# Sixteen feed-forward products ahead of the second group's norm, activations kept split for both column halves, last chunks staggered

## The reference, cut to what matters

```python
merged = sigmoid(ga) * (ya @ w_oa) + sigmoid(gb) * (yb @ w_ob)
x = x + merged @ w_out
h = rmsnorm(x, g_ffn)
a, u = split(h @ w_gu, 2, axis=-1)
x = x + (silu(a) * u) @ w_down
y = rmsnorm(x, g_final)
```

## Time and profile before

| | us |
|---|---|
| median of 3 runs (lowest, highest) | 1729.94 (1729.34, 1731.08) |
| the profiled execution | 1735.67 |
| its span, first to last instruction | 1733.9 |
| PE busy | 1653.6 (95%) |
| DVE busy | 953.3 (55%) |
| ACT busy | 662.3 (38%) |
| mean granted TensorE clock, share of full | 0.985 |

### The profile page before, as it was taken

The page is one execution under the profiler, slowest core; times in us unless marked ns, Lnnn a source line. Parts: engine busy times, 40 slices in busy tenths (PEclk is TensorE's granted clock), DMA queues, the critical chain, the costliest instruction groups (busy, mean ns, idle before and its releaser), DMA issues. The chain is left out here.

```text
span 1733.9 us, 27407 instructions
## 1 busy us (share of the span) xinstructions
PE 1653.6 (95%) x10688; PEld 1543.3 (89%) x10688; DVE 953.3 (55%) x2043; ACT 662.3 (38%) x1262; POOL 132.7 (8%) x235
## 2 busy tenths in 40 slices
PE   6999999999999999999998689999999999999997
PEld 6999999999999988888986689999999998787875
DVE  6546555654654634354564666666666664454444
ACT  5335444544544533342433422222222222334323
POOL 3001111000000001020010000000000002000000
PEclk9999999999999999999999889999999999999998
DMA  6142333455242345666461223222222228665643
GB/s 197 28 153 93 134 102 98 135 162 148 66 132 90 114 131 141 224 208 246 140 214 65 78 81 94 75 75 76 75 82 83 80 70 280 205 195 170 219 146 103
DMA packets 187824, 225.59 MB, mean 130 GB/s; under 512 B 13623, under 2 KB 135000, under 8 KB 187176
## 3 DMA queue, kind: packets, MB, share of 16 engines
q1 hardware_dynamic: 166608, 151.03, 29.2%
q0 software_dynamic: 21088, 72.81, 11.6%
HBM read 173.32 MB, written 50.54 MB: 129 GB/s over the span
## 5 line engine op out<-in xcount | busy, mean ns | idle before, releaser
L2021 PE MATMUL ps<-h_hi,w_hi 128*128 128x384 f32 (+1 forms) x816 | 275.0, 337 | 1.8 <-DVE w_lo L1366 1.1
L2023 PE MATMUL ps<-h_hi,w_lo 128*128 128x384 f32 (+1 forms) x816 | 267.9, 328 | 0.0
L2022 PE MATMUL ps<-h_lo,w_hi 128*128 128x384 f32 (+1 forms) x816 | 267.8, 328 | 0.0
L2021 PE MATMUL ps<-t_hi,e_hi 128*128 128x272 f32 x704 | 203.6, 289 | 10.6 <-DVE silu L1783 10.6
L2022 PE MATMUL ps<-t_lo,e_hi 128*128 128x272 f32 x704 | 203.6, 289 | 0.0
L2023 PE MATMUL ps<-t_hi,e_lo 128*128 128x272 f32 x704 | 202.8, 288 | 0.0
L2021 PE MATMUL ps<-b_hi,e_hi 128*128 128x272 f32 x528 | 155.0, 294 | 11.4 <-DVE e_lo L1768 11.4
L2021 PEld LDWEIGHTS ps<-h_hi,w_hi 128*128 128x128 f32 x816 | 155.1, 190 | 3.2 <-DVE w_lo L1366 1.4
L2022 PEld LDWEIGHTS ps<-h_lo,w_hi 128*128 128x128 f32 x816 | 155.0, 190 | 0.5 <-issue 0.5
L2023 PEld LDWEIGHTS ps<-h_hi,w_lo 128*128 128x128 f32 x816 | 154.6, 189 | 0.0
L2022 PE MATMUL ps<-b_lo,e_hi 128*128 128x272 f32 x528 | 154.3, 292 | 0.0
(11 more groups left out here) (320 smaller groups left out, 3554.4 us busy)
## 6 DMA issues: line engine op xcount, KB each, us to landing
w_raw<-in_w_gu_dram SPq DMA_DIRECT2D x96, 256.0 KB, 3.2
w_raw<-in_w_down_dram SPq DMA_DIRECT2D x88, 256.0 KB, 3.1
as_raw<-act_d SPq DMA_DIRECT2D x44, 512.0 KB, 4.7
w_raw<-in_w_in_dram SPq DMA_DIRECT2D x68, 256.0 KB, 3.3
zg_d<-stg POOLq DMA_DIRECT2D x28, 544.0 KB, 3.1
act_d<-act POOLq DMA_DIRECT2D x44, 272.0 KB, 2.7
w_raw<-in_w_out_dram SPq DMA_DIRECT2D x32, 256.0 KB, 3.7
gate<-zg_d POOLq DMA_DIRECT2D x8, 576.0 KB, 4.2
```

The costliest lines, as they stand in the source:

```text
L2021: nc.tensor.matmul(out, l_hi, r_hi, start=start, stop=False)
L2022: nc.tensor.matmul(out, l_hi, r_lo, start=False, stop=False)
L2023: return nc.tensor.matmul(out, l_lo, r_hi, start=False, stop=stop)
```

## The change

1. `FILL` goes from 4 to 8: sixteen products (P1 and P2 of f = 0 to 7) stand before P6 of f = 0. `p1` and `silu1` have eight buffers; to make room `sum2`, `sum3`, `col12`, `col22` have one each and `col21` goes (P4 adds straight into `act1`).
2. The sums of group 1's tiles are cut in pieces (`sums_first`, `sums_second`, `sums_hi(o, which)`, `sums_lo(o, which)`) and put between the sixteen products, one piece a product. The splits of products 2 and 3 stand ahead of the first tile's sums.
3. In `out_second` the turn of group 0's tile c stands in the middle of chunk c and its copies in iteration c; the left residual is added in two parts around the split of chunk 5.
4. Chunks 6 and 7 of w_out, and 42 and 43 of w_down, are staggered: chunk 6 of three tiles, chunk 7 of the same three, then both of the fourth and of the fifth.
5. `as_hi` and `as_lo` have eleven places and stay for the right half of the columns: 22 loads and splits of activations in place of 44.
6. `x1f`, `new_raw` and `gfin_row` are loaded behind given chunks of `ffn_out`, not in one burst; the split of `new_raw` moves from chunk 12 to 16.

```diff
-FILL = 4
-PRODUCTS = [("P1", 0), ("P1", 1), ("P2", 0), ("P2", 1), ("P1", 2), ("P1", 3), ("P2", 2), ("P2", 3)]
+FILL = 8
+PRODUCTS = [(_p, _f + _k) for _f in range(0, FILL, 2) for _p in ("P1", "P2") for _k in range(2)]
...
+def next_splits(q):
+    n = 2 * FILL
+    if n - RING <= q < n:
+        return {n - 3: (n,), n - 2: (n + 1, n + 2), n - 1: (n + 3,)}.get(q, ())
+    return (q + RING,) if q + RING < NQ else ()
...
 (POOL, ffn_out)
-            pool.wait_ge(sem("e_used"), NQ)
...
+            for t in range(4):
+                after_chunk(1 + 2 * t)
+                pool.dma_start(x1f[0][:, t, :], x1_d[t]).then_inc(sem("x1_landed0"), 16)
...
+                after_chunk(10 + k)
                 pool.dma_start(new_raw[:, :, 32 * k:32 * k + 32], act_d[:, :, HALF * k + 512:HALF * k + HALF].rearrange("b p t -> p b t")) \
...
+            for t in range(5):
+                after_chunk(12 + t)
...
 (ScalarE, end of out_second and ffn_in)
                 product_hi(0)
                 product_hi(1)
-                sums_hi(0)
-                std_d1(4)
+                sums_hi(0, range(4))
                 product_hi(2)
                 product_hi(3)
-                direct_hi(1)
-                product_read(0)
-                product_hi(4)
-                sums_hi(1)
...
+                std_d1(4)
...
+                beside = {0: lambda: direct_hi(1), 3: lambda: direct_hi(2), 7: lambda: direct_hi(3), 10: lambda: direct_hi(4)}
+                sums = {0: (1, (0, 1)), 1: (1, (2, 3)), 4: (2, (0, 1)), 5: (2, (2, 3)), 8: (3, (0, 1)), 9: (3, (2, 3)),
+                        11: (4, (0, 1)), 12: (4, (2, 3))}
+                for q in range(2 * FILL):
+                    if q in beside:
+                        beside[q]()
+                    if q in sums:
+                        sums_hi(*sums[q])
+                    for ahead in next_splits(q):
+                        product_hi(ahead)
+                    product_read(q)
...
 (VectorE, out_second)
                 for c in range(7):
-                    split_lo(b + c + 1, (c + 1) % 2)
-                    if 1 <= c < 5:
-                        operands_d0(c - 1)
-                    if 1 <= c < 3:
-                        scale_d0(c + 1)
                     if c == 4:
                         v.wait_ge(sem("x1_landed1"), 16 * 5)
-                        residual(1, 0, x1, D_BANKS[1], b + 4 - NB, "d1_x1")
+                        residual(1, 0, x1, D_BANKS[1], b + 4 - NB, "d1_x1", (0, 1))
+                    split_lo(b + c + 1, (c + 1) % 2)
+                    if c < 4:
+                        operands_d0(c)
+                    if c < 2:
+                        scale_d0(c + 2)
+                    if c == 4:
+                        residual(1, 0, x1, D_BANKS[1], b + 4 - NB, "d1_x1", (2, 3, 4))
...
 (VectorE, its end, and ffn_in)
                 product_lo(0)
                 product_lo(1)
-                sums_lo(0)
+                sums_lo(0, range(4))
                 scale_d1(2)
...
+                product_lo(2)
+                product_lo(3)
...
+                def beside(q):
+                    if q in (0, 4, 8, 11):
+                        sums_first((1, 2, 3, 4)[(0, 4, 8, 11).index(q)])
+                    elif q in (1, 5, 9, 12):
+                        o = (1, 2, 3, 4)[(1, 5, 9, 12).index(q)]
+                        sums_second(o)
+                        sums_lo(o, (0,))
+                    elif q in (2, 6, 10, 13):
+                        sums_lo((1, 2, 3, 4)[(2, 6, 10, 13).index(q)], (1, 2, 3))
+                    elif q in (3, 7):
+                        scale_d1(3 if q == 3 else 4)
...
+                for q in range(NQ):
+                    beside(q)
+                    if q and PRODUCTS[q - 1][0] == "P3":
+                        second_act(PRODUCTS[q - 1][1])
...
+                    product_read(q)
+                    for ahead in next_splits(q):
+                        if PRODUCTS[ahead][0] == "P6":
+                            weight_sums(PRODUCTS[ahead][1])
+                        product_lo(ahead)
...
 (ScalarE and VectorE, ffn_out)
-                        if m >= 1:
-                            act_hi(m + 1)
+                        if m and (m + 1) % 22 < 11:
+                            act_hi((m + 1) // 22, (m + 1) % 11)
...
 (TensorE)
-                pe.wait_ge(w_lo_done, CH_D[1] + 8)
-                for o, (t, R) in enumerate(last_tiles):
...
+                for o, c in ((0, 6), (1, 6), (2, 6), (0, 7), (1, 7), (2, 7), (3, 6), (3, 7), (4, 6), (4, 7)):
+                    pe.wait_ge(w_lo_done, CH_D[1] + c + 1)
...
-                turns_before = {0: 1, 2: 2, 5: 3, 7: 4}
+                turns_before = {0: 1, 2: 2, 5: 3, 9: 4}
...
+                for t, m in ((0, 42), (1, 42), (2, 42), (0, 43), (1, 43), (2, 43), (3, 42), (3, 43), (4, 42), (4, 43)):
+                    pe.wait_ge(w_lo_done, N_CHUNKS + m + 1)
```

More of the change, by code:

```diff
@@ L317, in build_program @@
         assert H0 - 16384 == H0 - 2 * 8192
[L318 to L334, removed]
@@ L335, in build_program, with temps @@
-        new_parts = place("new_parts", [P, NFF, P], F32R, at=H0 + 78336)
-        yf = place("yf", [P, 5, D], at=H0 + 89600)
-        gfin_row = place("gfin_row", [P, D], at=H0 + 110080)
+        def temps(name, places):
+            return [place(f"{name}_{k}", [P, 2, HALF // 2], at=H0 + at) for k, at in enumerate(places)]
+        p1 = temps("p1", (168192, 120832, 104448, 108800, 113152, 172544, 176896, 181248))
+        silu1 = temps("silu1", (170368, 123008, 106624, 110976, 115328, 174720, 179072, 117504))
@@ new lines, in build_program @@
+        sum2, sum3, col22, col12 = (temps(n, (142592 + 2176 * k,))[0] for k, n in enumerate(("sum2", "sum3", "col22", "col12")))
+        act1, act2 = (temps(n, (142592 + 2176 * (4 + 2 * k), 142592 + 2176 * (5 + 2 * k))) for k, n in enumerate(("act1", "act2")))
+        as_hi = place("as_hi", [P, 11, 2, 512], F32R, at=H0 + 8192)
+        as_lo = place("as_lo", [P, 11, 2, 512], F32R, at=H0 + 53248)
+        as_raw = place("as_raw", [P, 2, 2, 512], at=H0)
+        x1f = [place("x1f0", [P, 4, D], at=H0 + 98304), place("x1f1", [P, 5, D], at=H0 + 114688)]
@@ L339, in build_program @@
+        new_raw = place("new_raw", [P, NFF, DEC], at=H0 + 135168)
+        new_parts = place("new_parts", [P, NFF, P], F32R, at=H0 + 140800)
+        yf = place("yf", [P, 5, D], at=H0 + 152064)
+        gfin_row = place("gfin_row", [P, D], at=H0 + 180736)
         ps = ctx.enter_context(nc.psum_tensor("ps", [P, 8, 512], F32))
@@ L900, in _, with after_chunk @@
                         .then_inc(sem(f"act_saved{f % 2}"), 16)
-            pool.wait_ge(sem("e_used"), NQ)
[L902 to L906, removed]
+            def after_chunk(m):
+                pool.wait_ge(w_used, N_CHUNKS - NB - 2 + m + 1)
+            for t in range(4):
+                after_chunk(1 + 2 * t)
+                pool.dma_start(x1f[0][:, t, :], x1_d[t]).then_inc(sem("x1_landed0"), 16)
             for f in range(2):
@@ L1196, in direct_hi, with sums_hi @@
                     nc.scalar.copy(b22_hi[:, :, P * (o - 1):P * o], bank_view(bank + 1, P)).then_inc(sem("t_hi_done"), 1)
-            def sums_hi(o):
+            def sums_hi(o, which):
                 cols, w = (slice(512, HALF), 32) if o == 0 else (slice(P * (o - 1), P * o), P)
-                for k in range(4):
+                for k in which:
                     a.wait_ge(sem("t_sums"), T_SUMS[o] - 3 + k)
@@ L1247, in product_read @@
                     a.wait_ge(sem("e_read"), D_COUNT["P3", f])
-                    nc.scalar.activation(col12[f % 2][:, :, :], col12[f % 2][:, :, :], ACT.Silu).then_inc(sem("e_act_read"), 1)
+                    nc.scalar.activation(col12[:, :, :], col12[:, :, :], ACT.Silu).then_inc(sem("e_act_read"), 1)
             def out_first():
@@ L1868, in residual_tile, with residual @@
                 nc.vector.tensor_tensor(part, ps[0:R, bank, :], part, ALU.add).then_inc(sem(name), 1)
-            def residual(g, half, x1, banks, used, name):
+            def residual(g, half, x1, banks, used, name, tiles=None):
                 t0, nt = GROUPS[g][:2]
                 v.wait_ge(w_used, used)
-                for t in range(nt):
+                for t in tiles or range(nt):
                     residual_tile(x1, rows_of(t0 + t), t, half, banks[half][t], name)
@@ L2299, in tile_product, with token_chunk @@
                 return nc.tensor.matmul(ps[:, bank, :], l_hi, r_lo, start=False, stop=stop)
-            def token_chunk(banks, tiles, first, last_k, stationary, slot, wait=None):
+            def token_chunk(banks, tiles, first, last_k, stationary, slot, wait=None, between=None):
                 hi, lo = v2(w_hi, slot), v2(w_lo, slot)
                 for q in range(2):
+                    if q and between:
+                        between()
                     for t, R in tiles:
@@ L2455, in wait_of @@
                     return wait
-                for m in range(44):
```

(1 more changed line is left out.)

209 lines of the change are left out of this document (87 added, 122 removed).

## The result

The kernel after takes 1692.28 us (median of four runs, 1688.43 to 1692.98) beside 1730.51 for the kernel before (1729.34 to 1732.58): a ratio of 0.9773 [0.9755, 0.9791]. A second set of four runs gave 1692.09 and 0.976 [0.9747, 0.9774]. The profiled execution took 1691.97 us with a span of 1690.2, against 1735.67 and 1733.9 before; its mean granted clock is 0.994, where it was 0.985.

What follows compares the result with a forecast made beforehand. TensorE, busy 95% of the span, was taken as the bound through its waits and half-clock stretches. Gains 6.6 + 22.5 + 15.5 = 44.6 us took 1735.7 to 1691.1, less 5.7 gave 1685; range 1675 to 1703.

Steps and rivals of the forecast that it cites:

- The places: Out_second, the eight products beside the sums, and ffn_out: nearly all idle time after attention, about 42 us, plus 15 of clock.
- Out_second: Out_second, turns moved and chunks 6 and 7 staggered: waits of 2.90 and 2.45 go, 1.4 comes; 6.6 us gained.
- The sixteen products: Product 0 to P6 of f = 0: takes 57.0 us against 80.1 counted for before; gain taken as 22.5 us.
- the landing of the load for f = 2: Before product 2: load issued at 953.7 lands at 959.0; wait 2.9 us (1.3 to 4.7), clock falls once, 1.5 us.
- Rival (a): Products before P6: engine lists become the bound, each pair ends late, clock falls; about 8 us cost, 1693 us; chance 0.22.
- Ffn_out: Ffn_out, activations kept, loads paced, last chunks staggered: waits for activations shrink or go; 15.5 us gained.
- the first chunks' waits: First chunks of ffn_out: three waits for as_lo during the burst of loads go; 6.2 us and 1.6 of clock.
- the 3.67: Ffn_out before chunk 42: the 3.67 us wait for as_lo goes through the stagger, with 1.6 of clock.
- 1.47 and 1.61: Ffn_out, residual waits at chunks 22 and 33: 1.47 stays; 2.75 becomes 1.55, gaining 1.2 us and 1.6 of clock.
- Rival (e): Ffn_out: new_raw or x1f loads now hold up w_down, 2 us a chunk over four or five; 1696 us; chance 0.07.
- the sum: Ffn_out's parts added: 6.2 + 1.6 + 2.8 + 5.3 - 0.4 = 15.5 us.
- my last step: Whole kernel: 5.7 us, the profiled execution's distance above the median, taken off 1691.1 to give 1685.3, stated as 1685.

Runs made afterwards that it cites:

- experiment 4: Kernel before with one edit: VectorE splits the weights of products 2 and 3 before the first tile's sums; 1729.25 us, ratio 0.9994.

## Why the prediction was right, and what was off

The places held and the mechanisms but for one step, and 44.6 us forecast for the profiled execution stand against 43.7 measured. Both numbers start from the same execution of the kernel before, 1735.67, so the agreement says more of the working than of the typical gain, which is 38.2 between medians.

*Out_second* held step by step: a new wait of 1.37 in chunk 0 (1.4 forecast), 1.34 before product 0 (1.8 forecast), the clock up throughout; 6.9 for 6.6.

*The sixteen products*: the step that failed is the landing of the load for f = 2. I had it at 5.3 us after its issue with an upper bound of 7.1; it took 7.6, outside both, and the wait is 5.05, not 2.9. I counted 1.2 MB of stores and 0.5 of the load at 408 GB/s. There were 1.3 MB of stores, moved at 328 GB/s until the load's first packet, 3.9 us after its issue; then 1.0 MB, since the load for f = 3 goes out with that for f = 2, at 291. Where no stores are under way (the kernel before, the one without stores) the first packet comes 1.0 us after the issue. So of the 3.8 us by which the load was later than in the kernel before, 2.9 are its start behind the stores and 0.9 the time in which it moved together with its successor. Counting bytes at the best rate seen was no bound. The Trainium skill's page "DMA: Bandwidth & Descriptors" (Queues, rings and completion order) says that a DMA engine takes its queues in turn, packet by packet. From that I had made half of the rate from the start and a landing at 5 us. This trace doesn't agree: 362 packets of the stores and none of the load in 3.9 us. Why the load had no turn here stays open; in ffn_out, where the prediction held a landing of 14.3 us against the rule, packets did go in turn, as the last section shows. Small steps cancelled part of the miss: product 15 doesn't wait (0.8 forecast, at most 0.36 in the second trace), P6 waits 0.91 for 0.7. And the clock fell as forecast, once, for 6.8 us of which PE worked in 3.9. Rival (a) was not what happened: no wait between product 2 and P6 reached 0.25 us, 0.4 in the second trace.

*Ffn_out* held but for its parts' shares: the first chunks' waits and the 3.67 are gone, 1.47 and 1.61 stay (1.55 forecast for the second), and the last add starts 0.65 us behind PE's end, 0.25 later than before (0.4 forecast). Rival (e) didn't happen: loads of the new tokens' pieces, 18.0 us in the burst, now take 6.1 at the median. The stretch gave 1.1 us more than the sum; as that is less than the 2.6 us by which two traces of the same code differ there (experiment 4), no part need hold it.

*The median.* 1685 was forecast and 1692.28 measured, in the range, 7.3 off: 0.9 from the terms, 0.3 since the profiled run lay that much below its median, 0.3 from rounding, and 5.7 is my last step, the distance by which before's profiled execution lay above the median of its three runs. It is no constant, as the 0.3 after shows. The other sets have the kernel before at medians of 1733.46, 1731.6 and 1733.44, over 1725.65 to 1737.01 in 31 runs; 1735.67 is near the top of that spread (four runs were slower), and 1729.94 was at its lower side. Without that step the forecast would have been 1691.1, 1.2 us off, and that would have been luck in part: a gain read from one long execution and taken off its own time.

## What to carry to other kernels

When instructions of three engines are interleaved by hand, the cost of a late transfer shows at whatever stands behind its first reader in some list; find the load, then see what else the DMA is given at that moment. Spread bulk stores as their tiles are finished and loads as their consumers advance: here the two bursts cost some 4 and 6 us, and the first met the load only since the change had moved the split before it forward. Work on an engine that is half idle need not be saved: the 22 loads and 44 splits less bought nothing measurable.

## What the runs showed of the hardware

- The 512 KB load for f = 2 took 3.8 us in the kernel before, 4.4 to 4.6 with the stores gone or over, and 7.6 behind 1.3 MB of stores on POOL's queue (7.4 to 7.6 in the eight other traces that have the stores there). It moved no packet before the stores were nearly through, 3.9 us after the issue (3.9 to 4.0 in those eight). In the burst of ffn_out one of the same size took 15.6. There the queues do go packet by packet. The kernel before, 1456 to 1467:

```profile
q0 software_dynamic: 829, 3.00, 67.2%
q1 hardware_dynamic: 831, 1.57, 37.1%
```

  POOL's loads get two thirds of the bytes, as their packets are larger (3.6 KB on the mean, SP's 1.9). In the fill the packets of the load are 0.5 KB and q0 holds stores; whether such a difference matters wasn't tried.
- The loads of the new tokens, whose pieces are 128 bytes long, took 18.0 us in the burst before and 6.1 paced (medians).
- The forecast let waits up to 1.5 us pass and had the clock fall from 2.45 on. Between them the length of a wait alone doesn't decide. The clock fell behind 1.77, 1.78, 1.85, 1.97, 1.99, 2.39 and 2.51 us, and not behind 1.87, 1.92, 2.04, 2.57 and 2.60. The 2.57 stands in the kernel before, at 1471.08, and the prediction passed over it. The wait of 2.45 before chunk 7 lowered the clock there (933.01) and not in the reordered kernel (935.02). Two of the others, from the windows of the kernel with early stores (behind 1.77) and of the reordered kernel before (behind 2.60):

```profile
956.60:959.00 2.40, 2.40 (x14) 0.68 0.19 54
```

```profile
1467.90:1471.00 3.10, 3.10 (x14) 1.00 1.01 361
```

- The kernel before varied by 11.4 us over 31 runs on three chips (0.7%).
